# The maximum over a sample's scores in the cross-attention: transposes on VectorE, or on TensorE

## What is computed

```
hn = rms_norm(x, norm_x_pre)
q  = einsum("bsd,dhe->bshe", hn, w_xq)
s  = einsum("bshe,bmhe->bhsm", q, mem_k) * MEM_SCALE
p  = softmax(s, axis=-1)
o  = einsum("bhsm,bmhe->bshe", p, mem_v)
x  = x + rms_norm(einsum("bshe,hed->bsd", o, w_xo), norm_x_post)
```

## Time and profile before

| | |
|---|---|
| median of 3 runs | 1199.14 us (1198.11 to 1199.17) |
| the profiled execution | 1199.14 us, of which its span is 1197.5 us |
| TensorE busy | 1147.5 us (96%) |
| VectorE busy | 894.9 us (75%) |
| ScalarE busy | 643.2 us (54%) |
| GpSimd busy | 172.8 us (14%) |
| DMA | 216.13 MB, mean 180 GB/s |

### The profile page before, as it was taken

One profiled execution on the slowest core, in us unless ns is written; L12 is line 12 of the kernel. 1 busy time (PEld: TensorE's weight loads), 2 busy tenths in 40 slices (PEclk: granted clock), 3 DMA queues, 4 the chain that ended last, 5 costly groups with the idle time before them and its releaser, 6 DMA issues. The chain is left out here.

```text
span 1197.5 us, 25816 instructions
## 1 busy us (share of the span) xinstructions
PE 1147.5 (96%) x10203; PEld 1059.9 (89%) x10203; DVE 894.9 (75%) x1527; ACT 643.2 (54%) x1130; POOL 172.8 (14%) x282
## 2 busy tenths in 40 slices
PE   6999999999999999998879999999999999999988
PEld 6999999999777899987869999999986779999877
DVE  5689988889767544677587998888897674448756
ACT  7474454545457444565565645444545664446554
POOL 1210101010353000032011010101014520001310
PEclk9999999999999999999989999999999999999999
DMA  7795756475568466687447766665754765667852
GB/s 214 187 263 142 220 137 179 121 187 135 167 188 239 140 186 179 188 249 269 119 117 195 201 174 188 163 164 138 187 146 138 219 195 157 181 189 215 266 206 73
DMA packets 318971, 216.13 MB, mean 180 GB/s; under 512 B 21620, under 2 KB 300512, under 8 KB 318298
## 3 DMA queue, kind: packets, MB, share of 16 engines
q1 hardware_dynamic: 301728, 164.64, 50.1%
q0 software_dynamic: 16800, 49.83, 13.2%
q10 hardware_dynamic: 330, 0.11, 0.0%
HBM read 209.31 MB, written 7.15 MB: 181 GB/s over the span
## 5 line engine op out<-in xcount | busy, mean ns | idle before, releaser
L1329 ACT ACTIVATE whi<-stage 128x2048 fp32r<-128x2048 f32 (+2 forms) x157 | 272.9, 1739 | 277.7 <-PE U L691 233.0
L1951 DVE TENSOR_TENSOR wlo<-stage,whi 128x2048 fp32r<-128x2048 f32 x138 | 315.8, 2288 | 130.2 <-ACT whi L1329 130.1
L689 PE MATMUL U<-Ahi,whi 128*128 128x264 f32 x1152 | 333.5, 290 | 1.4 <-DVE wlo L1951 0.8
L690 PE MATMUL U<-Alo,whi 128*128 128x264 f32 x1152 | 327.0, 284 | 0.0
L691 PE MATMUL U<-Ahi,wlo 128*128 128x264 f32 x1152 | 326.5, 283 | 0.0
L689 PEld LDWEIGHTS U<-Ahi,whi 128*128 128x128 f32 x1152 | 217.3, 189 | 5.4 <-DVE wlo L1951 1.7
L690 PEld LDWEIGHTS U<-Alo,whi 128*128 128x128 f32 x1152 | 217.5, 189 | 0.0
L691 PEld LDWEIGHTS U<-Ahi,wlo 128*128 128x128 f32 x1152 | 216.4, 188 | 0.0
L2128 DVE SCALAR_TENSOR_TENSOR acc<-uext,cwall,acc 128x256 f32<-128x256 f32 x464 | 189.2, 479 | 0.4
L689 PE MATMUL U<-Bhi,whi 128*128 128x264 f32 x384 | 109.1, 284 | 0.0
L690 PE MATMUL U<-Blo,whi 128*128 128x264 f32 x384 | 108.9, 284 | 0.0
(11 more groups left out here) (460 smaller groups left out, 2171.8 us busy)
## 6 DMA issues: line engine op xcount, KB each, us to landing
stage<-in_w_in SPq DMA_DIRECT2D x76, 1024.0 KB, 6.0
stage<-in_w_out SPq DMA_DIRECT2D x32, 1024.0 KB, 5.8
stage<-in_w_mk SPq DMA_DIRECT2D x8, 1024.0 KB, 6.2
cp<-in_cache_kv_latent POOLq DMA_DIRECT2D x64, 128.0 KB, 3.1
cp<-in_cache_kv_latent SPq DMA_DIRECT2D x64, 128.0 KB, 2.9
stage<-in_w_mv SPq DMA_DIRECT2D x8, 1024.0 KB, 5.4
Kt<-in_cache_mem_k POOLq DMA_DIRECT2D x16, 512.0 KB, 6.9
stage<-in_w_xq SPq DMA_DIRECT2D x8, 1024.0 KB, 7.1
```

Source lines behind the costliest of these rows:

```text
L689: mm(bk[:, 0:cols], whi[:, s, w], hi[:, k, :], start=(k == 0), stop=False)
L690: mm(bk[:, 0:cols], whi[:, s, w], lo[:, k, :], start=False, stop=False)
L1329: return A_(out, in_, ACT.Copy, scale=scale)
L1951: ins = V.tensor_tensor(wlo[:, s, :], stage[:, s, :], whi[:, s, :].bitcast(F32), ALU.subtract)
```

## The change

The two transposes on VectorE go, with the `memset` and the four blocks `yTurn`. In their place TensorE makes one transpose (`y_max_turn`): the column of 128 row maxima, `sm[:, 10:11]`, becomes one row of 128 in the PSUM bank `U[1]`. VectorE takes the maximum over the four quarters there and writes 128 values on one partition, `ymax`. TensorE makes a column of them again, by a product with a one (`y_max_back`). VectorE multiplies that column, read from PSUM, by the negative scale. Two semaphores have five counts per layer where they had three. Both TensorE functions stand behind `x_values(3)`.

```diff
--- before.py
+++ after.py
@@ -51,7 +51,7 @@
 U_KPE, U_HEAD, U_MK, U_OUT, U_MV, U_XQ, U_XO = 6, 8, 40, 44, 60, 64, 68
 NST = 2
 
-CHAIN_LAYER = 340
+CHAIN_LAYER = 336
 
 
 class Count:
@@ -229,7 +229,7 @@
     qm = at("qm", [P, 4, MH, NB, 32], W)
     doX = at("doX", [R, MD], W + 16384)
     same = at("same", [P, MH * NB], W + 41728)
-    yTurn = [at(f"yTurn{i}", [P, 32], A0 + 33024 + 128 * i) for i in range(4)]
+    ymax = at("ymax", [1, P], A0 + 33024)
 
     pm = at("pm", [P, 2, MH, NB, NB], B1 + MH * T * 4)
     dX = at("dX", [P, 2 * 32], A0 + 32768)
@@ -317,9 +317,9 @@
         C(n, MH) for n in ("xs_mm", "xm_rdy", "xex", "xp_rdy", "xT_mm", "xT_ev", "xv_mm", "xv_ev"))
     kb_rdy, ys_mm = C("kb_rdy", NB), C("ys_mm", NB)
     qm_rdy, yex, yo_ev = (C(n, 1) for n in ("qm_rdy", "yex", "yo_ev"))
-    ym_dve, ym_pe = C("ym_dve", 3), C("ym_pe", 3)
-    YM_BIAS, YM_PROBS, YM_RECIP = 1, 2, 3
-    YM_QUERY, YM_KEYS, YM_SUM = 1, 2, 3
+    ym_dve, ym_pe = C("ym_dve", 5), C("ym_pe", 5)
+    YM_ROW, YM_ALL, YM_BIAS, YM_PROBS, YM_RECIP = 1, 2, 3, 4, 5
+    YM_QUERY, YM_TURN, YM_BACK, YM_KEYS, YM_SUM = 1, 2, 3, 4, 5
     xr_rdy = C("xr_rdy", 2)
     yo_mm = C("yo_mm", 2)
     xo_hi, xo_lo = C("xo_hi", MH + 1), C("xo_lo", 1)
@@ -1207,6 +1207,16 @@
                                   start=(b + eb == 0), stop=(b == NB - 1 and eb == 3))
                 last.then_inc(ys_mm.sem, 1)
 
+            def y_max_turn():
+
+                pe.wait_ge(ym_dve.sem, ym_dve.at(l, YM_ROW))
+                tr(U[1][0:1, 0:P], sm[:, 10:11], ident[:, :]).then_inc(ym_pe.sem, 1)
+
+            def y_max_back():
+
+                pe.wait_ge(ym_dve.sem, ym_dve.at(l, YM_ALL))
+                mm(U[1][:, P:P + 1], ymax[:, :], ones[0:1, 0:1], start=True, stop=True).then_inc(ym_pe.sem, 1)
+
             part(U_XQ + 1, 1, *XB, 0, 4)
             combine(7, 5)
             part(U_XQ + 1, 1, *XB, 4, KC)
@@ -1236,6 +1246,8 @@
             x_transposes(3)
             y_scores(7)
             x_values(3)
+            y_max_turn()
+            y_max_back()
 
             pe.wait_ge(mt_ev.sem, mt_ev.at(l, 8))
             wait_apart(pe, yex.sem, yex.at(l, 1))
@@ -2578,22 +2590,17 @@
             x_max(3)
             x_out(1)
             key_blocks(5)
-            V.memset(yTurn[0][:, :], 0.0)
             x_recip(3)
             key_blocks(6)
             x_out(2)
             key_blocks(7)
             dve.wait_ge(ys_mm.sem, ys_mm.at(l, NB))
-            ch.step(V.tensor_reduce(yTurn[0][:, 0:1], ST[:, 0:64], AX, ALU.max))
-            ch.wait()
-            ch.step(V.transpose(yTurn[1][:, :], yTurn[0][:, :]))
-            ch.wait()
-            ch.step(V.tensor_reduce(yTurn[2][:, :].rearrange("p (i b) -> p i b", i=4), bc(
-                yTurn[1][:, :].rearrange("p (i b) -> p b i", i=4).unsqueeze(1), [P, 4, NB, 4]), AX, ALU.max))
-            ch.wait()
-            ch.step(V.transpose(yTurn[3][:, :], yTurn[2][:, :]))
-            ch.wait()
-            V.tensor_scalar(sm[:, 8:9], yTurn[3][:, 0:1], -MSCALE, None, ALU.mult).then_inc(ym_dve.sem, 1)
+            V.tensor_reduce(sm[:, 10:11], ST[:, 0:64], AX, ALU.max).then_inc(ym_dve.sem, 1)
+            dve.wait_ge(ym_pe.sem, ym_pe.at(l, YM_TURN))
+            V.tensor_reduce(ymax[:, :].rearrange("p (h i b) -> p h i b", h=MH, i=4), bc(
+                U[1][0:1, 0:P].rearrange("p (h i b) -> p h b i", h=MH, i=4).unsqueeze(2), [1, MH, 4, NB, 4]), AX, ALU.max).then_inc(ym_dve.sem, 1)
+            dve.wait_ge(ym_pe.sem, ym_pe.at(l, YM_BACK))
+            V.tensor_scalar(sm[:, 8:9], U[1][:, P:P + 1], -MSCALE, None, ALU.mult).then_inc(ym_dve.sem, 1)
             dve.wait_ge(ym_pe.sem, ym_pe.at(l, YM_KEYS))
             dve.wait_ge(m_zero.sem, m_zero.at(l, 2))
             V.tensor_copy(pm[:, :, :, :, :].rearrange("p t h b c -> p t h (b c)")[:, :, :, 0:NB * NB:NB + 1],
```

## The result

The changed kernel is slower, by more than forecast. Its runs have a median of 1204.01 us (1202.68 to 1209.15) beside 1198.12 us for the kernel before; the ratio is 1.0052, 95% interval 1.0034 to 1.0069. Run again in two later comparisons it gave 1.0042 (1.0029 to 1.0056) and 1.0041 (1.0024 to 1.0057). So it costs 5 to 6 us, where 3.6 were forecast. Three executions that are not in that median took 1201.51, 1202.09 and 1205.12 us; with them the median of nine is 1203.53. The profiled execution is the first of these, the quickest of the nine.

What follows compares the result with a forecast made beforehand. TensorE, busy 96% of the span, was taken as the bound, so only its stops count. From the queued start, 0.27 + 1.02 + 0.39 + 0.16 + 0.20 gave +1.80 us per layer: 1199.14 + 3.6 = 1202.7 us, 8-in-10 range 1200.9 to 1204.0.

Steps and rivals of the forecast that it cites:

- The turn waits behind the prompt values: TensorE's transpose of the row maxima queues behind the prompt values, starting 1.07 us after them; 0.9 us of waiting.
- The maximum over the quarters: VectorE's maximum over 512 elements on one partition, from PSUM: 1.02 us, bounds 0.68 and 1.12.
- The way back: TensorE's product turning the row of 128 into a column again: 0.39 us, bounds 0.20 and 0.60.
- The scaling: VectorE's multiplication of the column, read from PSUM, by the negative scale: 0.16 us.
- The handovers: Four passes between engines, from the turn to the exponentials, at 0.05 us each: 0.20 us.
- The chain: From the start of the maximum to ScalarE's exponentials: 1.80 us longer per layer, between 1.23 and 2.1.
- The low clock ends sooner between the layers: Rival: TensorE's half-clock stretch after the layer turn ends earlier, up to 1.7 us back, total 1201.0 us; chance 0.12.
- The clock falls in the longer stop: Rival: more TensorE idle time slows the sample values, 1.7 us per layer, total 1206.1 us; chance 0.05.
- Another bubble: Rival: added instructions move layer 1's unnamed TensorE stop among late sample scores, up to 1.1 us either way; chance 0.07.
- No part of it comes back later: TensorE's 9.40 us stop between the layers, waiting on VectorE's residual, moves with the rest and hides nothing.

Runs made afterwards that it cites:

- the kernels that hold the clock: The changed kernel, and the kernel before with a longer VectorE maximum chain, each with three wide idle products per layer in TensorE's stops: ratio 1.0024 each.
- half of the delay: The kernel before with one more VectorE maximum of 128x512 elements ahead of the scaling, nothing added on TensorE: ratio 1.0018.
- the two instructions: The kernel before with a transpose and a product on constants behind the prompt values, read by nothing: ratio 0.9998.
- the two kernels with 13 and 15 short ones: Idle 128x128 transposes in TensorE's stops: 13 per layer in the changed kernel, 1.0026; 15 in the kernel before with a longer VectorE chain, 1.0031.
- the kernel with the turn first: The changed kernel with the transpose of the row maxima put ahead of the last prompt head's values in TensorE's order: ratio 1.0009.

## Why the prediction was wrong, step by step

The direction and the main mechanism were right. The size was not: 1204.01 us against a forecast of 1202.7 and an upper end of 1204.0. Two errors of opposite sign met, a chain taken as 1.0 us too long over both layers and a loss by the clock of some 2 us that was no part of the sum. The kernel before, too, came out 1.0 us lower beside the changed one than the 1199.14 us that the forecast started from. That the forecast came as near as it did is luck.

- *The turn waits behind the prompt values*: right. Forecast 1.07 us after their start, measured 0.97. Put ahead of them it saves 0.64 us per layer. The forecast's 0.9 us of waiting is the distance from the row maximum's end to the turn, and not what a better order gives back, since then the values stand ahead of the way back.
- *The maximum over the quarters*, 1.02 us: mis-sized, it took 0.68. I scaled the old step with its access of every eighth element in SBUF, 371 ns for 128. Here, read from PSUM on one partition, this access costs nothing extra: 680 ns is what the contiguous 512 elements took the earlier trace rows. Memory and number of partitions both differ from the old step, and no run tells which of them takes the extra away. The formula of the Trainium skill (VectorE: DVE Perf Modes, section "The TRN2 errata — SBUF-src ops pay a fixed extra latency per instruction"), stated there for an fp32 add of two tensors, gives an estimate of 0.69 us, and the trace agrees. I had that figure beside the row and chose the row.
- *The way back*, 0.39 us: 563.34 - 562.96 = 0.38. *The scaling*: 0.16, as forecast. *The handovers*, 0.20 in all: 0.04, 0.05, 0.04 and 0.03, so 0.16.
- *The chain*: forecast +1.80 per layer, measured +1.31, in all layers of all three profiles. Alone it would give 1.0022, and the kernels that hold the clock measure 1.0024.
- *The low clock ends sooner between the layers*, 0.12: nothing shows it, and it could not have paid. In the changed kernel's first profile the low clock between the layers lasted longer than before, until about 610.5 us and not 607.5. Still TensorE reached its next wait for VectorE, 8.11 us after the restart, at the same distance as before; only the wait was shorter, 0.87 instead of 1.77 us. The two others have 8.11 us too. Here VectorE sets the pace, and the 1.7 us that this rival wanted back were never lost. The first row is of the kernel before, where TensorE restarted at 604.08, the second of the changed one, where it restarted at 604.42:

```profile
612.19 0.39 PE L705 MATMUL U<-Ahi,whi 128*128 128x264 f32 x1 [1.77 <-DVE Alo L2518]
```

```profile
612.53 0.39 PE L705 MATMUL U<-Ahi,whi 128*128 128x264 f32 x1 [0.87 <-DVE Alo L2530]
```
- *The clock falls in the longer stop*, 0.05: this is the step that failed. I called it unlikely since the single stops stay below 2 us, far from the 9.40 between the layers. The single stops from the last scores to the sample values were even shorter, 0.77 us at most, and the clock fell all the same in 4 of 6 layers. So the forecast's sum had nothing for it, and the longest stop was the wrong thing to look at: with half of the delay the longest stop was 1.28 us, and its two profiled layers have no fall. What the runs show in its place is that the whole thin stretch matters, a few short stops and small matmuls together: with wide products in the stops none of four profiled layers had a fall. The price was well chosen: forecast 1.7 us per layer, measured 1.27 to 1.67, some 2.1 us per execution. I weighed it at 0.05 when it came in 4 of 6 layers.
- *Another bubble*, 0.07: not from the two instructions (0.9998). In the two kernels with 13 and 15 short ones the stop in layer 1 was 1.83 and 1.61 us.
- *No part of it comes back later*: right. The stop between the layers is 9.41 us after, 9.40 before.

The Trainium skill (TensorE: Matmul & The Clock Gate, section "HAM oscillation — how this bites in real kernels") names idle gaps as what brings the clock down. The trace agrees in kind, with the single stops of 9.40 us between the layers and 3.58 us in the kernel with the turn first. The section's warning is of one long gap, and here the clock also fell where the gaps were several short ones.

What stays open: how far the chain can grow without a fall (half of the delay gave 1.0018, and the one profile shows none), why one layer has the fall and another with the same instructions has not, and the unnamed stops among the sample scores.

## What to carry to other kernels

A step moved to another engine waits behind what that engine has queued: price it from the point where the queue lets it start, and try it ahead of the queue. Where a chain that TensorE waits for gets longer, count the whole thin stretch around it, not the longest stop: the matmuls behind it may run at half clock; here the loss was about twice what the chain shows. A few wide matmuls on constants in the stops test this in one run. Look also at what follows a stretch at the lower clock: between the layers TensorE waits for VectorE soon after it, and there the stretch cost nothing.

## What was not expected of the hardware

The clock fell with no stop of TensorE above 0.77 us between the last sample scores and the sample values. Some 6 us ahead of the sample values, among the scores, there is the unnamed stop. It was 0.68, 0.96, 1.41 and 0.53 us in the four layers with a fall and 0.72 and 1.18 in the two without, so it does not tell them apart. At this place the clock did not fall where the chain was 2.02 us long or less (in profiles of five kernels, ten layers, and the kernel before), and it fell in 6 of 8 layers where it was 2.6 us or more without idle work.

A maximum over every eighth element took 371 ns for 128 elements in SBUF, 85 more than a contiguous one of that size (286 ns), and 680 ns for 512 in PSUM on one partition, the same as contiguous on 128.
